# The MLP as one written-out product of 64 units, and the mixer's last products that split their own operand tiles

## The reference, cut to what matters

```python
merged = merged + gate * (branches[i] @ w_branch_up[i])      # for four branches
x = x + rms_norm(merged @ w_out, norm_mix_post)
h2 = rms_norm(x, norm_mlp_pre)
u = jax.nn.relu(h2 @ w_mlp_in)                                # 1024 -> 4096
x = x + rms_norm((u * u) @ w_mlp_out, norm_mlp_post)          # 4096 -> 1024
...
mod = jax.nn.silu(c) @ mod_w[l] + mod_b[l]                    # 3072 outputs
shift, scale, gate = jnp.split(mod[:, None, :], 3, axis=-1)
mod_k = jax.nn.silu(c_ctx) @ mod_w[l] + mod_b[l]              # 2048 of them are used
h = rms_norm_2(x, norm_g[l]) * (1.0 + scale) + shift
...
yc = jnp.einsum('btc,ce->bte', jax.nn.silu(u), lp['c_pw']) + lp['c_pw_b']
p = pool_fn(dv)                                               # box means of 2, 4, 8, 16
yd = (jnp.einsum('btgi,gij->btgj', pg, lp['d_w']) + lp['d_b']).reshape(...) * lp['d_scale']
cat = jnp.concatenate([ya * jax.nn.silu(za), yb * jax.nn.silu(zb),
                       yc * jax.nn.silu(zc), yd * jax.nn.silu(zd)], axis=-1)
x = x + gate * jnp.einsum('bte,ed->btd', cat, lp['w_out'])
return rms_norm_2(x, final_g)
```

## Time and profile before

| what | value |
|---|---|
| median of 3 runs | 3168.24 us (3167.03 to 3168.61) |
| the profiled execution | 3166.92 us, of which its span is 3164.8 us |
| mean granted TensorE clock | 0.957 |
| PE busy | 2837.9 us (90%) |
| DVE busy, ACT busy | 1437.3 us (45%), 945.8 us (30%) |

### The profile page before, as it was taken

How to read it: one execution, slowest core, us unless ns; L and a number is a source line. 1 busy time by engine, 2 the same in 40 slices (tenths; PEclk the granted TensorE clock), 3 DMA queues, 4 the chain that set the end, 5 groups by cost and what they waited for, 6 DMA issues and landing times. The chain is left out here.

```text
span 3164.8 us, 35403 instructions
## 1 busy us (share of the span) xinstructions
PE 2837.9 (90%) x14648; PEld 2206.8 (70%) x14648; DVE 1437.3 (45%) x1577; ACT 945.8 (30%) x1212; POOL 93.8 (3%) x136
## 2 busy tenths in 40 slices
PE   6999998899889898896999999999399989997978
PEld 5767777577667676674788777878177768866756
DVE  2164442532231335736343433333646778833753
ACT  3141212332212534413332322121346622223022
POOL 0001110000000101000000000000000000000000
PEclk9989999999999999998999999999699999999989
DMA  2110101101111106511141322211220121113221
GB/s 103 50 64 32 38 32 51 64 28 54 49 46 68 48 12 227 166 40 73 63 136 54 127 73 87 67 47 40 120 74 27 47 80 54 47 47 114 76 107 66
DMA packets 65656, 221.21 MB, mean 70 GB/s; under 512 B 6984, under 2 KB 11880, under 8 KB 63856
## 3 DMA queue, kind: packets, MB, share of 16 engines
q1 hardware_dynamic: 54144, 177.85, 16.5%
q0 software_dynamic: 11376, 41.42, 3.8%
HBM read 180.45 MB, written 38.80 MB: 69 GB/s over the span
## 5 line engine op out<-in xcount | busy, mean ns | idle before, releaser
L275 PE MATMUL psum<-mixer_in,weights_parts 128*128 128x512 f32 x2112 | 504.2, 399 | 19.1 <-PEq L179 16.3
L275 PEld LDWEIGHTS psum<-mixer_in,weights_parts 128*128 128x128 f32 x2112 | 398.1, 189 | 118.4 <-issue 17.8
L414 PE MATMUL psum<-hidden,weights_parts 128*128 128x512 f32 x1536 | 435.2, 425 | 39.5 <-ACT early_gate L438 22.1
L242 DVE TENSOR_TENSOR weights_parts<-weights_raw,weights_parts 128x1024 fp32r<-128x1024 f32 (+2 forms) x195 | 211.4, 1084 | 415.1 <-ACT weights_parts L226 414.7
L275 PE MATMUL psum<-mlp_hidden,weights_parts 128*128 128x512 f32 x1536 | 360.9, 398 | 20.3 <-PEq L179 20.3
L414 PEld LDWEIGHTS psum<-hidden,weights_parts 128*128 128x128 f32 x1536 | 287.6, 196 | 126.4 <-issue 34.7
L275 PE MATMUL psum<-mlp_in,weights_parts 128*128 128x512 f32 x1536 | 356.1, 394 | 13.2 <-PEq L2401 8.4
L275 PEld LDWEIGHTS psum<-mlp_hidden,weights_parts 128*128 128x128 f32 x1536 | 293.6, 191 | 87.6 <-issue 21.9
L275 PEld LDWEIGHTS psum<-mlp_in,weights_parts 128*128 128x128 f32 x1536 | 290.0, 189 | 79.7 <-issue 15.2
L275 PE MATMUL psum<-hidden,weights_parts 128*128 128x512 f32 x1200 | 280.6, 397 | 11.3 <-PEq L795 6.6
L226 ACT CAST weights_parts<-weights_raw 128x1024 fp32r<-128x1024 f32 (+2 forms) x195 | 182.2, 934 | 308.9 <-PE psum L275 139.2
(11 more groups left out here) (442 smaller groups left out, 3066.0 us busy)
## 6 DMA issues: line engine op xcount, KB each, us to landing
weights_raw<-in_w_in SPq DMA_DIRECT2D x73, 512.0 KB, 3.5
squares<-in_mod_w POOLq DMA_DIRECT2D x40, 512.0 KB, 4.0
weights_raw<-in_w_gate SPq DMA_DIRECT2D x32, 512.0 KB, 3.8
gate_scratch<-early_gate SPq DMA_DIRECT2D x64, 256.0 KB, 2.2
gate<-gate_scratch POOLq DMA_DIRECT2D x32, 512.0 KB, 4.3
weights_raw<-in_w_mlp_in SPq DMA_DIRECT2D x32, 512.0 KB, 3.4
weights_raw<-in_w_mlp_out SPq DMA_DIRECT2D x32, 512.0 KB, 3.5
weights_raw<-in_w_out SPq DMA_DIRECT2D x24, 512.0 KB, 3.6
```

Of the source, the lines that this page charges most:

```text
L242: nc.vector.tensor_tensor(c.parts[:, s, 1, 0:w], c.raw[:, s, 0:w], c.parts[:, s, 0, 0:w].bitcast(F32), ALU.subtract).then_inc(c.low_ready, 1)
L275: mm = nc.tensor.matmul(c.psum[:, bank + h, 0:cols], c.parts[:, s, wp, at], moving(k, xp, h), start=(n < halves), stop=(n >= halves * (3 * ...
L414: mm = nc.tensor.matmul(c.psum[:, bank, :], c.parts[:, s, wp, at], self.hidden[:, k, xp, h * HALF:(h + 1) * HALF], start=(k == 0 and n == ...
```

## The change

`mlp` becomes one gemm of 64 units, wholly written out, with the weights of both matrices interleaved in one array `w_mlp`; a per-unit wait (`before_hidden`) guards each hidden tile, and `banks_read_at=0` frees a unit's banks after the first epilogue operation. `Modulation` has buffers of its own and works in half tiles of 512 columns, two a unit, in units 4 to 43. `add_residual` with `defer` no longer waits for its store; the first `y` copy of the MLP does. In `first_two` the second unit runs two tiles behind the first. The load of `mixed` goes to POOL's queue and runs beside `glu_product`; both last products use `lead` with `Splitting`, the second in the order 4 to 7, 0 to 3; the whole pooling branch is background of the first, its clearing is reduced to the borders, and the reload of the GLU result and of the final residual go to POOL's queue.

```diff
@@ gemm
-                        pe.wait_ge(c.dve_done, dve_count(u - 2, dve_per_unit - 1))
+                        last = dve_per_unit - 1 if banks_read_at is None else banks_read_at
+                        pe.wait_ge(c.dve_done, dve_count(u - 2, last))
...
-                for k in ks:
-                    lead(pe, k)
+                for i in range(kt + 2):
                     for u in range(2):
+                        if not 0 <= i - 2 * u < kt:
+                            continue
+                        k = ks[i - 2 * u]
+                        if u == 0:
+                            lead(pe, k)
@@ Modulation
+    HALVES = [(n, 0, h) for n in range(3 * KT) for h in range(NH)] + [
+        (n, 1, h) for n in range(2 * KT) for h in range(NH)]
+    FIRST = 4
...
+    def at(self, u):
+        first = NH * (u - self.FIRST)
+        return [(m, *self.HALVES[m]) for m in range(first, first + NH)
+                if 0 <= m < len(self.HALVES)]
@@ add_residual
-                    sp.wait_ge(c.scratch_stored, c.stored)
+                    if not defer:
+                        sp.wait_ge(c.scratch_stored, c.stored)
@@ mlp
-        for chunk in range(FF_CHUNKS):
-            gemm(nc, c, t["w_mlp_in"], KT, KT, lambda k, x, n: h[:, k, x, n * HALF:(n + 1) * HALF],
...
-            gemm(nc, c, t["w_mlp_out"], KT, KT,
...
+            if u < 2 * KT:
+                dve.wait_ge(c.scratch_stored, c.stored)
+                nc.vector.tensor_copy(y[:, k, :], result).then_inc(c.dve_done, 1)
...
+        def before_hidden(pe, q, k):
+            if q % (2 * KT) == KT:
+                pe.wait_ge(c.dve_done, hidden_done(q - KT + k))
+
+        def moving(k, x, n, q):
+            return (h if into(q) else u_parts)[:, k, x, n * HALF:(n + 1) * HALF]
+        gemm(nc, c, t["w_mlp"], units, KT, moving, act_per_unit=act_per_unit, act_epilogue=square,
+             dve_per_unit=dve_per_unit, dve_epilogue=keep, banks_read_by="dve", banks_read_at=0,
+             rhs_by_unit=True, unroll=units, then=(t["w_in_2"], 0, KT),
+             background={"dve": on_dve, "pe_inner": before_hidden, "pool": modulation.load,
+                         "act": lambda a, q, j: modulation.on_act(a, q)})
@@ glu_conv_branch, Pooling
-        with nc.Block() as block:
-            @block.sync
-            def _(sp):
-                load_residual(c, sp, x, t["cat"][0:KT].rearrange("n p s -> p n s"), False)
-        glu_product(nc, c, t, parts, u, gate)
+        glu_product(nc, c, t, parts, u, gate, load_mixed)
...
+        for step in {0: (0, 1, 2), 1: (3,), 2: (4,), 3: (5,), 4: (6,), 5: (7,)}.get(q, ()):
+            self.pool(v, step)
+        if q == MIX + 2:
+            self.finish(v, MIX - 1)
...
-        if q % 2 == 0 and q:
-            self.product(pe, q // 2 - 1)
+        if q in (1, 2, 3, 5):
+            self.product(pe, {1: 0, 2: 1, 3: 2, 5: 3}[q])
@@ mixer_out
-        split(nc, c, x, parts, wait=wait_residual,
...
+        product(0, copy, (t["w_out_2"], KT, KT), unroll=8, lead=pooling.splitting.ready,
+                background={"sp": store_glu, "act": pooling.on_act, "dve": pooling.on_dve,
+                            "pe": pooling.on_pe,
+                            "pool": lambda pool: pooling.load(pool, glu_dram)})
...
-        split(nc, c, tiles[:, 0:MIX, :], parts[:, MIX:, :, :])
-        split(nc, c, glu, parts, wait=lambda c, eng, k: eng.wait_ge(loaded, 16),
-              meanwhile=lambda sp: load_residual(c, sp, final, t["x_second"], False))
...
+                lead=splitting.ready, lead_order=splitting.order,
+                background={"act": splitting.on_act, "dve": split_and_clear,
+                            "pool": load_final})
```

More of the change, by code:

```diff
@@ L719, in begin @@
+        self.act = Steps(c, "act", sum([([f"silu{x}"] if m in (0, self.SECOND) else [])
+                                        + [f"summed{m}"] for m, (_, x, _) in enumerate(self.HALVES)], []))
+        self.vecs = Steps(c, "vec", [f"product{m}" for m in range(n)]
+                          + ["whole0", "whole1", "mod", "scale", "times", "plus", "gate"])
         self.act.end()
         self.vecs.end()
-        self.before = list(self.turns)
-        self.turns = [n + len(self.rows) // 2 for n in self.turns]
@@ new lines, in on_dve, with finish @@
+    def on_dve(self, v, u):
+        for m, n, x, h in self.at(u):
+            v.wait_ge(self.act.sem, self.act.value(f"silu{x}"))
+            v.wait_ge(self.loaded[m % 2], 16 * (m // 2 + 1))
+            w = self.w[:, m % 2, :]
+            self.nc.vector.tensor_tensor(w, w, self.row[:, h * HALF:(h + 1) * HALF],
+                                         ALU.mult).then_inc(self.vecs.step(f"product{m}"), 1)
+    def finish(self, v, u, times, plus, gate):
+        if u != self.FIRST + len(self.HALVES) // NH:
+            return
+        c, nc, vecs, mod = self.c, self.nc, self.vecs, self.sums[:, 0, :, :]
+        v.wait_ge(self.act.sem, self.act.value(f"summed{len(self.HALVES) - 1}"))
+        for x, n in ((0, 3 * KT), (1, 2 * KT)):
+            nc.vector.tensor_tensor(mod[:, 0:n, x], mod[:, 0:n, x], self.sums[:, 1, 0:n, x],
+                                    ALU.add).then_inc(vecs.step(f"whole{x}"), 1)
+        v.wait_ge(vecs.sem, vecs.value("whole1"))
@@ new lines, in on_dve @@
+        def on_dve(v, q, j):
+            if q == 0:
+                nc.vector.reciprocal(rstd, rstd).then_inc(vecs.step("rstd"), 1)
+                v.wait_ge(vecs.sem, vecs.value("rstd"))
+            if q == last:
+                v.wait_ge(c.dve_done, hidden_done(last - 1))
+                nc.vector.memset(total[:], 0.0).then_inc(cleared.step("zero"), 1)
+                v.wait_ge(cleared.sem, cleared.value("zero"))
+            modulation.on_dve(v, q)
+            modulation.finish(v, q, *modulated)
@@ new lines, in mlp, with hidden_done @@
+        act_per_unit = [2 if into(u) else int(u >= last) for u in range(units)]
+        dve_per_unit = [2 if into(u) or u >= last else 1 for u in range(units)]
+        d0 = c.base["gemm_dve"]
+        def hidden_done(u):
+            return d0 + sum(dve_per_unit[:u + 1])
+        def before_hidden(pe, q, k):
[3 more added lines that the diff above has]
+            return (h if into(q) else u_parts)[:, k, x, n * HALF:(n + 1) * HALF]
@@ L2650, in mix_out @@
         gemm(nc, c, t["w_out"], KT, KT, lambda k, x, n: parts[:, k, x, n * HALF:(n + 1) * HALF],
[L2651 removed]
+             then=(t["w_mlp"], 0, KT), lead=splitting.ready, **how)
         merged_ctx.close()
```

296 lines of the change are left out of this document (157 added, 139 removed).

## The result

The changed kernel takes 3094.88 us (median of 4 runs, 3094.46 to 3100.26), the kernel before 3167.64 us beside it on the same chip (3165.36 to 3168.61). The ratio is 0.9775, 95% interval 0.9758 to 0.9792. The forecast was 3094.

A forecast was written before the change was run, and what follows sets the result against it. PE, busy 90% of the span, was held by idle gaps and the lowered clock behind them. Terms 4.5 + 43.8 + 5.4 + 22.8 - 3.4 = 73.1 us, off 3166.9, gave 3093.8, stated as 3094; range 3085 to 3108, about 0.85.

The forecast's parts named there:

- the two new stalls: PE waits ahead of the first last product's third pooling product (3.3 us) and the last product's unit 2 (2.9 us).
- w_out: Product with w_out: a second unit two tiles behind shortens the wait for unit 2's weights and keeps the clock, 4.5 us.
- Start of the MLP: Ahead of the MLP: without the store's wait PE starts 6.9 us earlier; the first gemm keeps its clock, 3.5 us.
- Boundaries and clock: Inside the MLP: four 5.06 us and three 1.58 us gaps go, 25.0 us; w_mlp_out pieces keep their clock, 8.4 us.
- the four terms: The MLP's gains: earlier start 6.9, first gemm's clock 3.5, boundaries 25.0, w_mlp_out pieces' clock 8.4; together 43.8 us.
- The cover of the hidden tiles and of the modulation: In the MLP, late hidden tile 7 and modulation on DVE and ACT stay hidden behind matmuls; counted as 0.
- GLU: GLU product: 29.0 us becomes 23.6 without the block in front and the 4 MB on SP's queue, gain 5.4.
- Rival 3: Late POOL loads, DVE's pooling behind, or a clock drop at the MLP's start: 3 to 8 us, 3099; chance 0.10.
- First last product: From the GLU product's end to the second last product's start: 134.5 us becomes 111.7, gain 22.8.
- Last product: Last product: 91.02 us becomes 94.4, through a stall of 2.9 inside and two clock prices of 1.7; loss 3.4.
- Cadence: MLP's one piece draws a fast or slow matmul cadence once, 0 or 13.5 us; fast taken, three in four.
- rival 6: Anywhere in the MLP: straight-line fetching stalls PE, 73 us or more in all, 3186 at 30 ns a matmul; chance 0.02.

The follow-up runs named there:

- The three lags: Lead's second unit four tiles behind the first (3090.45 us) or none (3103.36 us), against the changed kernel's two (3094.88 us).
- whole-wait run: Changed kernel with the first unit over each hidden group waiting for all eight hidden tiles before its first matmul: 3125.55 us.
- 4 MB run: Changed kernel with the 4 MB load of `mixed` on SP's queue instead of POOL's, at the same place: 3101.78 us.
- 64-byte run: Changed kernel with a buffer of 64 bytes a partition in front of the MLP's tiles: 3106.64 us.
- store's run: Kernel before, with SP's wait for the 4 MB store gone and the first copy into `y` waiting instead: 3157.91 us against 3163.52.

## Why the prediction was right

Its mechanism held: the waits at the boundaries, the store and the queue were the price, and the two new stalls came where the sum put them, within 0.5 us. That the total is within 1 us of the forecast is luck. The parts below give 73.9 us where the span fell by 71.8: 2.1 us came back where the sum had no term, 0.9 between the product with `w_out` and the MLP, 0.9 between the MLP and the GLU product, 0.3 at the end. And about 3.2 us of the gain that the prediction put down to the clock were slow pieces of the one execution that it was reckoned from.

- **w_out: 4.5 summed, 4.3 found.** The gap is 0.90 us and the piece 66.20 instead of 67.78, from the rows above. The three lags confirm the working.
- **Start of the MLP: 10.4 summed.** The run with this edit alone gave 10.5 in the profile and 5.6 to 7.9 in the time. The 3.5 us that the sum takes for the clock are 1.8 of clock and 1.7 of cadence, by the first piece of the run with the loops written out; the sum was right because the fast cadence was drawn.
- **Boundaries and clock: 33.4 summed.** The whole-wait run puts back four gaps and their clock and nothing else. From the end of the residual to the end of the MLP it is 45.6 us less, where the four terms gave 43.8. What I missed is the fill and drain of a piece: 88.14 us is the length of one that stands alone, 87.89 that of one in a chain, and seven times the difference, for the seven boundaries that went, is 1.8. Of the 8.4 us for the clock some 1.5 were the slow cadence of the fourth piece, by the same run. The three waits of 1.58 us were put back by no run.
- **The cover of the hidden tiles and of the modulation** held: the page has no idle time ahead of `mlp_hidden`, and DVE still stands idle 3.9 us in a unit with modulation (over 3 in the prediction), as the timeline of DVE in the third piece shows (answering to the earlier trace rows):

```profile
1665.24 1.23 DVE L2598 SCALAR_TENSOR_TENSOR squares<-psum,square_totals 128x1024 f32<-128x1024 f32 x1 [3.93 <-PE psum L280]
```

- **GLU: 5.4 summed, 5.4 found** (29.0 to 23.6). The wait behind the 4 MB was 2.2 of it, the shorter boundary 1.3 (2.69 to 1.37), and most of the rest the clock: in the kernel before it was at 0.52 in the first unit (12.87 us, where 11.25 stand in the 4 MB run behind 1.37 us), as the window below shows. Rival 3, late loads on POOL's queue, did not come.

```profile
2885.00:2888.00 3.00, 3.00 (x8) 2.32 (x8) 0.69 (x1) 0.30 (x1) 0.00 (x0) 0.52 0.95 332
```

- **First last product: 22.8 summed, 22.3 found, but not term by term.** The stall was 2.88 for 3.3. The 1.7 us for the clock behind it were wrong here: it stayed at 1.00. It fell in other profiles behind the same wait of 2.7 to 2.9 us (the 4 MB run, and the 64-byte run, shown below). What made up for it: each piece between two pooling products costs 0.4 to 0.6 us of fill beside the 1.3 that I counted for the pooling product (48 matmuls take 11.40 us, 2900.72 - 2889.32, where 48 x 0.229 is 10.99), four times, and the last piece drew the slow cadence, 0.4 more. Pieces of this one product have both cadences, so it is not kept through a product, as the prediction has it, but can change where another product stands in between. No run puts the `split` blocks back; this term, the second in size, rests on the timelines.
- **Last product: -3.4 summed, -3.7 found**: a stall of 3.06 for 2.9, with the clock behind it as counted.
- **Cadence: the fast one, forecast at three in four, was drawn.** It was the likelier by more than I gave: in all seven profiles in which the MLP is unbroken and its tiles kept their place (the changed kernel and six experiments) it has 228.9 ns.

The 64-byte run around its third pooling product, timeline of PE:

```profile
2927.76 3.78 PE L3400 MATMUL psum<-pool_projected,pool_weights 128*128 128x512 f32 x4 [2.85 <-DVE pool_projected L3387]
2930.55 24.11 PE L280 MATMUL psum<-mixed_parts,weights_parts 128*128 128x512 f32 x96
```

and a window of it (columns as in the earlier trace rows), with the granted clock at 0.51:

```profile
2928.00:2934.00 6.00, 6.00 (x11) 3.37 (x12) 4.41 (x4) 0.00 (x0) 0.00 (x0) 0.51 0.56 174
```

Straight-line fetching did not cost anything (rival 6). The rule that I had set against the loops, from the Trainium skill, Runtime: NRT & Kernel Launch, "Instruction fetch mechanics", foresees a stall at a taken branch out of reach; the run with the loops written out does not show one (ratio 1.0001), so these bodies of two units do not fall under it. By the Trainium skill, SBUF — State Buffer, "SBUF: two separate sides", DVE's copies can hold back the descriptors of POOL's DMAs; the loads of `mixed` showed no such delay here, with no such copy beside them.

## What to carry to other kernels

Between two products, ask what the last unit's result still needs, and let only the first matmul that reads it wait for it: four boundaries of 5 us and the clock behind each were worth 28 us in the run that put them back. In a lead of two units, the lag of the second is to cover DVE's epilogue and the next weights' split; count it in matmuls, and look for the same lateness at each product that is written in. Before calling a difference in cadence chance, compare the SBUF addresses of the two operands of the matmul.

## What was new about the hardware

- The cadence of 128x512 matmuls with new weights each time, at a granted clock of 1.00, depends on the distance in SBUF between the weight tile and the moving tile: 228.9 ns at 64 modulo 128, 232.4 at 0, 233.3 at 96 (the only distances run; whether the period is 128 or more is not shown). Over 3072 matmuls the two slow ones cost 10.7 and 13.7 us.
- At the distance of 64 a piece still runs at 233.3 ns in some executions (the first long piece over `hidden` in the kernel before and in the changed one, the first `mlp_in` piece), and at 228.9 in others, of the same program. What draws it is open (so are the MLP's pieces in the store's run). At a distance of 96 no piece ran at 228.9. A product of 384 matmuls gains or loses 1.7 us by it, so it may be part of the spread between executions; the pieces of the executions without a profile are not seen, and this is only argued.
- The Trainium skill, TensorE: Matmul & The Clock Gate, "Wait — 56ns, not 53.3ns?", gives 215.7 ns for a back-to-back matmul of 512 columns at 2.4 GHz. No piece here came below 228.9 ns; with weights exchanged before each matmul the measurement decides.
- A wait of 2.5 to 2.9 us ahead of the third pooling product stands in nine profiles. It left the clock at 1.00 in seven of them and brought it to 0.5 in two, the 4 MB run (wait of 2.67 us) and the 64-byte run, there at a price of 2.9 us (24.11 instead of 22.56 us for the 96 matmuls, and 2.79 instead of 1.42 us from the start of the pooling product to theirs). My sum took 1.7 for such a drop and always.
